# Queries and keys as 512-column products in three attention stages of a two-block transformer kernel

## The reference

```python
q, k, v = h @ w_q, h @ w_k, h @ w_v              # h: 256 x 1024, each w: 1024 x 1024
z = einsum('bhtd,bhsd->bhts', q, k) * 64 ** -0.5 # 16 heads of 64
# stick: w[t,s] = exp(log_sigmoid(z) + sums over s < j < t of -softplus(z)), s < t
# moba:  w = softmax(z - slope[head] * distance), causal
# fox:   w = softmax(z + c[t] - c[s]), causal; c = running sum of log_sigmoid(h @ w_f + b_f)
y = einsum('bhts,bhsd->bhtd', w, v)
```

## Time and profile before

| | us |
|---|---|
| median of 3 runs | 1300.99 |
| lowest and highest of them | 1296.38, 1304.98 |
| the profiled execution, its own time | 1299.92 |
| its span (first to last instruction) | 1298.2 |

### The profile page before, as it was taken

One profiled execution on the slowest core, in us unless ns is written; L12 is line 12 of the kernel. 1 busy time (PEld: TensorE's weight loads), 2 busy tenths in 40 slices (PEclk: granted clock), 3 DMA queues, 4 the chain that ended last, 5 costly groups with the idle time before them and its releaser, 6 DMA issues.

```text
span 1298.2 us, 17757 instructions
## 1 busy us (share of the span) xinstructions
PE 1244.7 (96%) x6854; PEld 1056.2 (81%) x6854; DVE 821.1 (63%) x1276; ACT 638.4 (49%) x1016; POOL 190.5 (15%) x229
## 2 busy tenths in 40 slices
PE   5999999999999999999999999999999799999996
PEld 5788887898878878888878877888878787788885
DVE  4566666454676666666666766766554576776663
ACT  5344445565554445444456656444435464644342
POOL 1122220022030012222202310000000770000000
PEclk9899999999999999999999999999999899999999
DMA  6866554444745455666554445756552545566540
GB/s 203 269 192 194 190 183 141 131 114 130 238 151 195 162 163 161 191 193 192 189 164 138 124 159 176 248 172 202 177 162 66 159 145 170 191 213 204 185 162 33
DMA packets 175038, 221.77 MB, mean 171 GB/s; under 512 B 9709, under 2 KB 104537, under 8 KB 174697
## 3 DMA queue, kind: packets, MB, share of 16 engines
q1 hardware_dynamic: 173112, 213.20, 51.9%
q0 software_dynamic: 1536, 6.38, 1.5%
q10 hardware_dynamic: 304, 1.05, 0.2%
HBM read 219.53 MB, written 1.06 MB: 170 GB/s over the span
## 4 chain that ended last, share of the span: by engine, by line
PE 85%; DVE 6%; ACT 5%; DMA 2%; issue 1%; POOL 0%; SPq 0%; ACTq 0%; POOLq 0%; DVEq 0%
PE bank L1262 50%; PE bank L1344 19%; PE bank L1342 10%; DVE w_lo L848 2%; ACT w_hi L564 1%; PE bank L1453 1%; DMA raw<-in_ff_w_up 1%; ACT work L575 1%; ACT xt L590 1%; PE bank L1285 1%; PE bank L1440 1%; DVE xt L879 1%; PE bank L1418 1%; PE bank L1420 1%; DVE a_uv L1171 1%
## 5 line engine op out<-in xcount | busy, mean ns | idle before, releaser
L848 DVE TENSOR_TENSOR w_lo<-raw,w_hi 128x512 fp32r<-128x512 f32 (+1 forms) x496 | 508.2, 1047 | 213.3 <-ACT w_hi L564 211.2
L564 ACT ACTIVATE w_hi<-raw 128x512 fp32r<-128x512 f32 (+1 forms) x496 | 428.4, 896 | 249.6 <-DMA raw<-in_ff_w_up 88.0
L1344 PE MATMUL bank<-xt,w_hi 128*128 128x512 f32 x1216 | 436.0, 402 | 0.0
L1342 PE MATMUL bank<-xt,w_lo 128*128 128x256 f32 x1216 | 344.5, 283 | 9.2 <-DVE work L897 9.2
L1344 PEld LDWEIGHTS bank<-xt,w_hi 128*128 128x128 f32 x1216 | 230.9, 190 | 57.0
L1342 PEld LDWEIGHTS bank<-xt,w_lo 128*128 128x128 f32 x1216 | 232.1, 191 | 11.7 <-DVE w_lo L848 10.4
L1262 PE MATMUL bank<-w_hi,ht_lo 128*128 128x512 f32 x432 | 169.0, 391 | 7.4 <-DVE ht_lo L916 7.4
L1262 PE MATMUL bank<-w_lo,ht_hi 128*128 128x512 f32 x432 | 168.8, 391 | 0.0
L1262 PE MATMUL bank<-w_hi,ht_hi 128*128 128x512 f32 x432 | 168.6, 390 | 0.0
L1262 PE MATMUL bank<-w_hi,xt 128*128 128x512 f32 x512 | 160.8, 395 | 3.0 <-DVE w_lo L848 2.1
L1262 PEld LDWEIGHTS bank<-w_hi,xt 128*128 128x128 f32 x512 | 95.5, 189 | 26.0 <-issue 3.9
(11 more groups left out here) (179 smaller groups left out, 1192.7 us busy)
## 6 DMA issues: line engine op xcount, KB each, us to landing
raw<-in_w_up SPq DMA_DIRECT2D x64, 512.0 KB, 4.3
raw<-in_w_down SPq DMA_DIRECT2D x64, 512.0 KB, 4.4
raw<-in_ff_w_gate SPq DMA_DIRECT2D x88, 256.0 KB, 3.9
raw<-in_ff_w_up SPq DMA_DIRECT2D x88, 256.0 KB, 4.8
raw<-in_ff_w_down SPq DMA_DIRECT2D x88, 256.0 KB, 2.7
raw<-in_w_in SPq DMA_DIRECT2D x40, 512.0 KB, 4.4
raw<-in_w_in SPq DMA_DIRECT2D x32, 256.0 KB, 2.9
raw<-in_moba_w_qkv SPq DMA_DIRECT2D x32, 256.0 KB, 2.9
```

What stands on the lines that cost most here:

```text
L564: act.activation(w_hi[:, c % RING, 0:w], raw[:, c % RAW, 0:w], ACT.Copy).then_inc(s["hi_ready"], 1)
L848: dve.tensor_tensor(w_lo[:, c % RING, 0:w], raw[:, c % RAW, 0:w], w_hi[:, c % RING, 0:w].bitcast(F32), ALU.subtract).then_inc(s["lo_ready" ...
L1342: pe.matmul(up_bank[q][:, 0:S], w_l[:, k % 2, cols], xt_hi[:, k, :], start=k == 0, stop=False, skip_group_check=True)
L1344: ins = pe.matmul(up_bank[q][:], w_h[:, k % 2, cols], flat(xt[:, k, :, :]), start=False, stop=k == KT - 1, skip_group_check=True)
```

## The change

Queries and keys are projected with x_high and x_low side by side: for each of 8 row blocks one matmul of 512 columns, w_high times both halves of x, and one of 256 columns, w_low times x_high. The 512 columns fill a whole PSUM bank, and the two halves of the result are added by VectorE: `both` is a reduction over pairs, from 512 columns of PSUM to 256 of `q_sum` or `k_sum` in SBUF. A second instruction then multiplies by the norms: on VectorE for q, on VectorE for k in stick, and on GpSimd for k in moba and fox (`key`). For this the tile `xq` of fox is laid out like `xt`.

The weight units of q and k are 1,024 columns wide instead of 512: one unit for k and one for q, k first. A pair has 2 units instead of 4, so every `hi` and `lo` of these works on 1,024 columns, and their places in the queues of ScalarE and VectorE move.

On TensorE k is projected before q. Its first four row blocks come ahead of `scores(pr+1)`, the other four behind them, then `weighted(pr)`, and then all of q. VectorE takes k out ahead of `second_part(pr+1)` in stick, behind it in moba and fox. Two of the four units of the next stage that were prepared within the cycles are now prepared in the tail.

```diff
-            shapes += [(1024, 1)] * RING + [(512, 1)] * (4 * PAIRS)
+            shapes += [(1024, 1)] * (RING + 2 * PAIRS)
...
-        xq_hi = sb("xq_hi", [P, KT, S], F32R, scope=two)
-        xq_lo = sb("xq_lo", [P, KT, S], F32R, scope=two)
+        xq = sb("xq", [P, KT, 2, S], F32R, scope=two)
+        xq_hi, xq_lo = xq[:, :, 0, :], xq[:, :, 1, :]
...
-                def pair(c, i, pr):
-                    for n, w in enumerate((q_w, k_w)):
-                        for j in range(2):
-                            u = c + 2 * n + j
-                            room(u, i)
-                            send(u, i, slot(u, 4, 512), w[:, 4 * j:4 * j + 4, ds(pr * P, P)])
+                def pair(u, pr):
+                    for n, w in enumerate((k_w, q_w)):
+                        room(u + n, 0)
+                        send(u + n, 0, slot(u + n, 8, 1024), w[:, :, ds(pr * P, P)])
 
                 for u in range(RING):
                     room(b + u, 0)
                     e, j = divmod(u, 4)
                     send(b + u, 0, slot(b + u, 2, 1024), v_w[:, 2 * j:2 * j + 2, e * 512:(e + 1) * 512])
-                for i in range(0, PAIRS // 2):
-                    pair(b + RING, i, 2 * i)
-                    pair(b + RING + 4, i, 2 * i + 1)
+                for pr in range(PAIRS):
+                    pair(b + RING + 2 * pr, pr)
...
+            def key(phase, pr):
+
+                if phase == "stick":
+                    return
+                pool.wait_ge(s["k_sum"], at(phase, "k_sum") + pr + 1)
+                pool.tensor_tensor(kt[:, pr % 2, :], k_sum[:], rbc[:], ALU.mult).then_inc(s["kt_done"], 1)
+
             def pairs(phase):
                 if phase == "fox":
-                    pool.wait_ge(s["cn_done"], 1)
+                    key(phase, 0)
+                    key(phase, 1)
                 if phase != "stick":
                     biases(phase, 0)
                     biases(phase, 1)
                 for e in range(2):
+                    if phase == "moba":
+                        key(phase, e)
                     pair(phase, e, e, False)
                 for i in range(1, PAIRS // 2):
                     for e in range(2):
                         if phase != "stick":
                             biases(phase, 2 * i + e)
+                        key(phase, 2 * i + e)
...
                     second_part(pr, e)
-                    hi(c + 4)
                     first_part(pr + 1, 1 - e)
-                    hi(c + 5)
+                    hi(c + 2)
                     y_part(pr)
-                    hi(c + 6)
-                    hi(c + 7)
+                    hi(c + 3)
...
-                for u in range(8, 12):
+                for u in (8, 9):
                     hi(b + u)
                 values(1)
                 act.wait_ge(s["rbc_ready"], at(phase, "rbc_ready") + 1)
                 act.activation(rbc[:], rbc_bank[:, 0:S], ACT.Copy).then_inc(s["rbc_done"], 1)
-                for u in range(12, 16):
+                for u in (10, 11):
                     hi(b + u)
                 first_part(0, 0)
-                for u in range(16, 20):
+                for u in (12, 13):
                     hi(b + u)
                 for pr in range(PAIRS - 2):
-                    cycle(b + 16 + 4 * pr, pr, pr % 2)
+                    cycle(b + 12 + 2 * pr, pr, pr % 2)
                 second_part(PAIRS - 2, 0)
                 first_part(PAIRS - 1, 1)
+                hi(b + 26)
                 y_part(PAIRS - 2)
+                hi(b + 27)
...
-                def q_evac(c, i, e):
-                    consumed(dve, c + 1, i)
-                    dve.scalar_tensor_tensor(qt[:, e, :], q_bank[:, 0:S], float(DH) ** -0.5, rbc[:],
+                def both(dst, src):
+
+                    return dve.tensor_reduce(dst, src[:].rearrange("p (a b) -> p b a", a=2), AX_X, ALU.add)
+
+                def k_evac(c, pr):
+                    consumed(dve, c)
+                    if pr:
+
+                        dve.wait_ge(s["kt_done"], at(phase, "kt_done") + pr)
+                    both(k_sum[:], k_bank).then_inc(s["k_sum"], 1)
+                    if kind == "stick":
+                        dve.wait_ge(s["k_sum"], at(phase, "k_sum") + pr + 1)
+                        dve.tensor_tensor(kt[:, pr % 2, :], k_sum[:], rbc[:], ALU.mult).then_inc(s["kt_done"], 1)
+
+                def q_evac(c, pr):
+                    consumed(dve, c + 1)
+                    both(q_sum[:], q_bank).then_inc(s["q_sum"], 1)
+                    dve.wait_ge(s["q_sum"], at(phase, "q_sum") + pr + 1)
+                    dve.scalar_tensor_tensor(qt[:, pr % 2, :], q_sum[:], float(DH) ** -0.5, rbc[:],
                                              ALU.mult, ALU.mult).then_inc(s["qt_done"], 1)
-
-                def k_evac(c, i, e):
-                    consumed(dve, c + 3, i)
-                    dve.tensor_tensor(kt[:, e, :], k_bank[:, 0:S], rbc[:], ALU.mult).then_inc(s["kt_done"], 1)
...
                     first_part(pr + 1)
-                    lo(c + 4)
                     if kind == "stick":
-                        lo(c + 5)
-                        q_evac(c, 0, e)
+                        lo(c + 2)
+                        k_evac(c, pr + 2)
                     second_part(pr + 1)
                     if kind != "stick":
-                        q_evac(c, 0, e)
-                        lo(c + 5)
+                        k_evac(c, pr + 2)
                     y_part(pr)
-                    lo(c + 6)
-                    k_evac(c, 0, e)
-                    lo(c + 7)
+                    if kind != "stick":
+                        lo(c + 2)
+                    q_evac(c, pr + 2)
+                    lo(c + 3)
...
-                for u in (12, 13):
-                    lo(b + u)
+                lo(b + 9)
                 dve.wait_ge(s["rbc_done"], at(phase, "rbc_done") + 1)
-                q_evac(b + 8, 0, 0)
-                lo(b + 14)
-                lo(b + 15)
-                k_evac(b + 8, 0, 0)
+                k_evac(b + 8, 0)
+                lo(b + 10)
+                q_evac(b + 8, 0)
+                lo(b + 11)
+                k_evac(b + 10, 1)
                 if kind == "fox":
-                    q_evac(b + 12, 0, 1)
-                    k_evac(b + 12, 0, 1)
+                    q_evac(b + 10, 1)
                 first_part(0)
-                lo(b + 16)
+                lo(b + 12)
                 second_part(0)
                 if kind != "fox":
-                    q_evac(b + 12, 0, 1)
-                    lo(b + 17)
-                    k_evac(b + 12, 0, 1)
-                else:
-                    lo(b + 17)
-                lo(b + 18)
-                lo(b + 19)
+                    q_evac(b + 10, 1)
+                lo(b + 13)
                 for pr in range(PAIRS - 2):
-                    cycle(b + 16 + 4 * pr, pr, pr % 2)
+                    cycle(b + 12 + 2 * pr, pr, pr % 2)
                 first_part(PAIRS - 1)
                 second_part(PAIRS - 1)
+                lo(b + 26)
                 y_part(PAIRS - 2)
+                lo(b + 27)
...
-                def project(c, i, n):
-
-
-                    ready(c + n, i)
-                    dst, src = ((q_bank, xq), (k_bank, xkv))[n // 2]
-                    w = slot(c + n, 4, 512)
-                    for k in range(4 * (n % 2), 4 * (n % 2) + 4):
-                        ins = three(dst[:, 0:S], [v[:, k % 4, :] for v in w], part(src, k, slice(0, S)),
-                                    k == 0, k == KT - 1)
-                    ins.then_inc(s["used"], 1)
+                def project(c, n, half):
+
+                    if half == 0:
+                        ready(c + n)
+                    dst, src = ((k_bank, xt), (q_bank, xq_both))[n]
+                    high, low = slot(c + n, 8, 1024)
+                    ks = range(4 * half, 4 * half + 4)
+                    for k in ks:
+                        pe.matmul(dst[:], high[:, k, :], flat(src[:, k, :, :]), start=k == 0, stop=False,
+                                  skip_group_check=True)
+                    for k in ks:
+                        ins = pe.matmul(dst[:, 0:S], low[:, k, :], src[:, k, 0, :], start=False,
+                                        stop=k == KT - 1, skip_group_check=True)
+                    if half:
+                        ins.then_inc(s["used"], 1)
+
+                def project_pair(c):
+                    for n in range(2):
+                        for half in range(2):
+                            project(c, n, half)
...
-                def cycle(c, i, pr, e):
+                def cycle(c, pr, e):
                     middle(pr, e)
+                    pe.wait_ge(s["k_sum"], at(phase, "k_sum") + pr + 2)
+                    project(c, 0, 0)
                     scores(pr + 1, 1 - e)
-                    project(c, i, 0)
-                    project(c, i, 1)
+                    project(c, 0, 1)
                     weighted(pr, e)
```

(31 more changed lines are left out.)

13 lines of the change are left out of this document (7 added, 6 removed).

## The result

The changed kernel takes 1319.2 us (median of 4 runs, 1315.5 to 1322.6), the kernel before 1302.6 in the same comparison: a ratio of 1.0134, 95% interval 1.0108 to 1.0160. The forecast was 1318, from a kernel before taken at 1299.9 us: 18.3 us more, where the two medians lie 16.7 apart (14 to 21 by the interval). The profiled execution of the changed kernel has a span of 1320.5 us, 22.3 more than before.

A forecast was written before the change was run, and what follows sets the result against it. The prediction took TensorE, busy 96% of the span, to bound the kernel's cycles. Stick +10.5, moba +5.2 and fox +2.6 made 18.3 us on 1299.9, forecast 1318 us, range 1304 to 1328.

The forecast's parts named there:

- Stick: Stick stage: a longer chain from scores to middle makes TensorE wait 1.6 us per cycle; with the opening +10.5 us.
- Moba: Moba stage: opening +2.8, clock +1.7, cycles +0.2 and tail +0.5, together +5.2 us.
- the clock's price: Moba's opening: after TensorE's 3.4 us wait the granted clock falls, adding 1.7 us.
- The tail wait: Tails of moba and fox: only middle covers q's reduction and multiplication, +0.5 us each.
- slack 0.4, so no wait: Moba and fox cycles: lo ends 6.5 us after scores, TensorE needs it at about 6.9, so no wait.
- each cycle gets one more change ... 0.1 a cycle: Splitting k around scores: one more fp32/float32r change, 0.1 us a cycle (bounds 0 and 0.2), 1.8 us over 18 cycles.
- The cycle's +0.04: Moba's cycles: the split gives back what the projections save, +0.04 us a cycle.
- Fox: Fox stage: later first bias +0.6, hi and lo before the scaling +0.9, cycles +0.6, tail +0.5, together +2.6 us.
- The products: Projections of q and k: new matmul widths save 0.03 us each (bounds 0 and 0.10), 1.4 us over 48.
- The clock did not fall in stick: Rival: stick's 1.6 us waits also lower the clock, three to seven falls, +5 to +12 us, about 1326; chance 0.20.
- The chain was not shorter: Rival: stick's chain is shorter, 0.9 us a cycle or less, and moba's wait leaves the clock alone; 1309; chance 0.22.
- TensorE as the bound of the cycles: Rival: TensorE stays the bound everywhere, stick's masks are ready in time; 1294 us, faster; chance 0.08.

The follow-up runs named there:

- two runs: Changed kernel with k_evac of pair 1 behind first_part(0) at moba's opening, 1316.7 us; changed kernel with 14 unused matmuls filling moba's opening wait, 1322.0 us.
- The last version: The version with the tails, and in the cycles of moba and fox VectorE takes lo of the k unit ahead of y_part: 1297.6 us (0.9989).
- all queues mended: Changed kernel with four queue orders at once (stick's VectorE queue, moba's opening, fox's opening, lo(b+12) behind second_part(0) in all openings): 1301.4 us (1.0011).
- The version with the tails: The kernel with all queues mended, and q of the last pair ahead of weighted in the last cycle of moba and fox: 1299.5 us (0.9992).
- the run of the products alone: Kernel before, with the new 512- and 256-column products, reduction and multiplication in stick only, q taken out behind second_part: 1300.3 us (1.0004).
- the run with moba's opening mended: Changed kernel with k_evac of pair 1 behind first_part(0) at the opening of moba: 1316.7 us (1.0116).
- the one with moba's `scores` first: The version with the tails plus GpSimd's vn copy ahead of key in moba, and scores ahead of both k halves in moba's cycles: 1304.1 us (1.0034).

## Why the prediction was right, and which of its steps were not

**Stick, right.** Forecast +10.5, measured +10.25: waits of 1.50 to 1.55 where 1.6 was said, 7 times, the cycle 11.19 where 11.13 was said. The sum of intervals held in its parts: 2.42 us to `hi` (2.39), 3.28 from `hi` to the second part (3.24), 1.18 from there to TensorE (1.2). Undoing the queue order took 11.6 us from the stage. The clock stayed at 1.00 behind all seven waits.

**Moba, right in sum, wrong in one step.** The wait is 3.40 as forecast, the clock's price 10.10 - 8.50 = 1.6 (forecast 1.7), and two runs took it away. The opening came out at +2.6 (2.8) ahead of the first `middle`. The tail wait is 0.94 where the term was 0.5: the reduction of q starts only 0.57 us behind `middle`, since a slow `lo` stands ahead of it on VectorE. The step that failed is the slack: "slack 0.4, so no wait". `lo` took 1.66, not the 1.14 of its interval, since it meets GpSimd's `key`, and ends 6.80 us after `scores` (forecast 6.5), while k could start at 6.72 (forecast 6.9). So every cycle waits 0.2 us for `w_lo`. It did not show in the time because another step was too dear by as much: "each cycle gets one more change ... 0.1 a cycle". By rows, k in two halves takes 3.16 and q 2.91, 6.07 for both, where the kernel before needed 6.05 and the products save 0.11: the split costs 0.13. But k starts 0.57 behind `middle`, where `scores` started 0.77 behind it in the kernel before, a gain of 0.2. The cycle's +0.04 was a right number from two errors that cancel, which is luck. The last version shows it: with the wait gone and the split in place moba's cycles are 8.30, 0.17 shorter than in the kernel before.

**Fox, a little short.** Forecast +2.6, measured +3.1: the wait +1.5 (0.6 + 0.9), of which the later first bias is 0.5 (0.6), cycles +0.6 (0.6), tail +1.0 (0.5). The cycles' number is luck too: it was put down to the layout of `xq`, but with that layout and `lo` out of `key`'s way the cycle is 8.29, as in moba. What cost was the same slow `lo`. GpSimd's multiplication of 256 columns takes 0.74 where 0.9 was taken. Not seen in the forecast: that `lo` in front of the scaling binds the first head to both, which cost more than the change itself but was there before.

**The products.** 0.055 a projection, term 0.03, inside its bounds of 0 and 0.10. With all queues mended the changed kernel's cycles behind the first are 9.40, 8.30 and 8.29, where the kernel before has 9.53, 8.47 and 8.32 to 8.44, and the three stages take 213.0 us in the last version where they took 215.4. The time of that version is 1.5 us shorter, which is within its uncertainty. Waits are left: at the ends of stages, 0.67 us for `w_lo` in moba's first cycle, and in fox the 1.46 for `kt`. The version with the tails has the same order on GpSimd and not that wait; in the last one the bias steps on GpSimd ahead of `key` (lines 447 and 453) take 2.18 and 1.89 us where they took 1.17 and 1.41. Why was not tried.

**The rivals.** The clock did not fall in stick (1.00 over the stage). The chain was not shorter (7.83 us). TensorE as the bound of the cycles is what the kernel with mended queues became, at 1297.6 to 1301.4 and not at 1294: the openings kept their waits, and the products save 0.055 and not 0.10.

## What to carry to other kernels

When work is moved ahead of the point from which a chain starts, add up the chain again: it loses that cover, and the same queue order that was free becomes the bound. In a queue written by hand, ask of each instruction in front of a late one not only how long it runs but for whom it waits. And a longer way out of PSUM costs nothing in a cycle that has other work to put beside it, but is waited for where nothing covers it: 0.94 us in two tails, 1.34 and 1.52 at the two ends of stick in the run of the products alone.

## What was not expected of the hardware

The granted clock did not go by the length of the wait before it alone. (The first 15 us are left out here: it stayed at 1.00 there behind waits of up to 4.9 us.) In the kernel before it fell behind waits of 2.11 and 2.40 us in ff1 and stayed at 1.00 behind two of 2.14 us in the feed-forward layers of the second block. In the changed kernel it fell behind 1.86, 1.95, 3.04 and 3.40 us and behind one of the two of 2.14, and stayed at 1.00 behind all waits of 1.5 us in stick. In the run with moba's opening mended it stayed at 1.00 behind 1.68 us, and in the one with moba's `scores` first it fell behind 1.69. So the 1.6 us of the forecast's rival were nearer to a fall than 1.25 and 2.40 let it seem. Two stretches of the kernel before, behind 2.11 and behind 2.14 us, and one of the run with `scores` first, 2 us behind its wait of 1.69:

```profile
52.10:56.10 4.00, 3.96 (x15) 0.62 0.27 75
961.50:965.50 4.00, 3.98 (x18) 1.00 0.35 93
```
```profile
708.20:710.20 2.00, 2.00 (x8) 0.50 0.82 241
```

Behind the 8.21 us wait of fox the clock was already down during the wait: 0.78 over 1034 to 1041.5, 0.50 behind it.

Float32r matmuls start 0.57 us behind the start of moba's `middle` (fp32, 6 merged), fp32 `scores` 0.77 behind it. Why was not tried.

Of VectorE's `lo` and GpSimd's `key`, the one that starts second is longer by most of what is left of the first (0.45 and 0.90 us above); a difference of 0.17 us in the start decided which of the two paid.
